# A cast of weights, a low part and a pair of transposes put earlier or later at the entry to the up-projection of block two

## The chip, the cores and the metric

The kernel runs on one core of a Trainium2 chip. The metric is the device time in microseconds (us), the median of three runs. All rows come from one profiled execution. TensorE is called PE here, its weight loads PEld, VectorE DVE, ScalarE ACT, GpSimd POOL and SyncE SP, as in the rows.

## The reference, cut to what matters

The program is a two-block transformer on 256 tokens of width 1024 in float32. Block two has two layers, and each of them ends with a cross-attention to a memory and an MLP:

```
h = rms_norm_2(x, g[2])
y = memory_cross_attention(h, mem, xa_wq[l], xa_wkv[l], xa_wo[l], xa_mem_norm[l])
x = x + rms_norm_2(y, g[3])
h = rms_norm_2(x, g[4])
y = sq_relu_mlp(h, mlp_w1[l], mlp_w2[l])     # square(relu(h @ w1)) @ w2, 1024 -> 4096 -> 1024
```

The entry is the stretch from the cross-attention's last product, with `w_o` (256 x 1024), to the first products with `mlp_w1`. It runs twice, once for each layer. Between the two products lie a norm of `y`, an addition to `x`, and a turning (transposition) of `x`, since PE needs the features on the partitions.

## The kernel before

**Numbers and weights.** A float32 product is computed as three products of reduced float32 (fp32r): high by high, high by low, low by high. So each weight and each activation is split: ACT casts the high part, and DVE (for some halves POOL) subtracts it to get the low part. Weights stream from HBM through three raw buffers in chunks of 128 x 2048, each handled as two halves of 128 x 1024. Half `m` gets its high part in slot `m % 4` of `whi` (`HL` is 4), its low part in the same slot of `wlo`. ACT does the casts of the halves strictly in order: `split_half(k)` casts all halves up to number k that aren't cast yet. A cast into a slot must wait until PE has used up the half that was there before:

```
if m >= HL:
    act.wait_ge(pe_out, 2 * (m - HL + 1))
nc.scalar.copy(whi[:, m % HL, 0:w], raw[...]).then_inc(hi_done, 1)
```

PE adds two to `pe_out` for each half of weights that it has used up. With `n0` the first half of the job `out2`, the halves are: `n0 + 10, 11` for `w_q`; `n0 + 12, 13` for `w_o`; `n0 + 14, 15` for the first 256 columns of `mlp_w1` (step 0); `n0 + 16, 17` for the next 256 (step 1). Half `n0 + 16` takes the slot of half `n0 + 12`.

**Tokens.** The 256 tokens are two tiles (`tt` 0 and 1) of 128, and the 1024 features are eight blocks of 128, taken as four groups (`g` 0 to 3) of two.

**PE.** `cross_out(tt, c)` computes tile tt, columns 512c to 512c+511 of `y`, with six products: for each half `h` of `w_o` the lines L1997, L1998 and L1999. `w_o` is needed for all four of (0,0), (0,1), (1,0), (1,1), so only the last of them gives its halves back. In (1,1) the products L1998 and L1999 with half h add one each to `pe_out`, so half `n0 + 12` is given back by the third of the six products, and `n0 + 13` by the sixth:

```
if tt == c == 1:
    m0.then_inc(pe_out, 1)
    m1.then_inc(pe_out, 1)
```

Then comes `first_up()`. In it `turn_to(tt, g)` transposes two blocks of `x` (L1323, two instructions) once DVE has added that half of the tile's row to `x`; `spare` issues fillers (L1329); `high(step, tt, g, fs)` issues the products of high weights with both parts of the activations (L2034; two blocks of features for each block of 128 columns in `fs`); `low_weights(step, g)` those of the low weights (L2044). `high` of step 0 waits for `grp_dve`, which tells that DVE has made group g's low part, and `high` also for the cast of its half. `turn_to(1, 0)` and `turn_to(1, 1)` use the PSUM banks of groups 2 and 3 of tile 0, so they come behind those groups' low parts.

**ACT.** `cross_square(tt, c)` (L2645) sums squares of `y` for the norm; it waits for PE's product of that piece. `up_hi(tt, g)` (L2653, two instructions) makes the high part of a turned group.

**DVE.** `gain(tt, c)` (L3651) multiplies `y` by its gain and waits for the square of the same piece; `mean(tt)` (L3656) joins both sums of squares of a tile, for which POOL then takes the root (L939); `add(tt, c)` (L3662) adds the normed piece to `x`; `up_lo(tt, g)` (L3670, two instructions) makes the low part of a turned group out of `up_hi`'s result.

**POOL** behind the two roots: it waits for the last addition to `x`, loads a row of gains, and makes the low parts of halves `n0 + 16, 17` (L949). **SP** issues a chunk's load when both parts of the chunk three before have been made.

Every engine works through its list in the order of the code; nothing is reordered at run time.

Of the kernel before, what the change touches and what calls it, by code (L numbers as in the profile page):

```python
# [204 lines left out]
def build_network(nc, a, out):  # L205
# [66 lines left out]
    with ExitStack() as ctx:  # L272
# [843 lines left out]
        def _(pe):  # L1116
# [607 lines left out]
            for l in range(DEPTH):  # L1724
# [286 lines left out]
                def first_up():  # L2011

                    def turn_to(tt, g):

                        pe.wait_ge(x_ready, x_count("yx", l) - 3 + 2 * tt + g // 2)
                        turn_blocks(("xm", l, tt, g), [x[:, tt, (2 * g + b) * P:(2 * g + b + 1) * P] for b in range(2)])

                    def weights(step, g):

                        m = 2 * plan.jobs["w1", l, step][0] + g // 2  # L2020
                        return m, [w[:, m % HL, :].rearrange("p (k n) -> p k n", k=KD // 2) for w in (whi, wlo)]

                    def high(step, tt, g, fs=(0, 1)):

                        m, (wh, _) = weights(step, g)
                        if tt == 0 and g % 2 == 0:
                            pe.wait_ge(hi_done, m + 1)
                        if step == 0:
                            pe.wait_ge(grp_dve, plan.by_number[plan.groups["xm", l, tt, g]][2])
                        rows_ = slice(tt * P, tt * P + P)  # L2030
                        for f in fs:
                            both = ps[:, step_bank(step) + f, :].rearrange("p (i n) -> p i n", i=2)[:, :, rows_]
                            for k in (2 * g, 2 * g + 1):
                                nc.tensor.matmul(both, wh[:, k % 4, f * P:f * P + P], act2[:, k, :, rows_], start=k == 0 and tt == 0, stop=False)  # L2034

                    def low_weights(step, g):

                        m, (_, wl) = weights(step, g)
                        if g % 2 == 0:
                            wait_lo(pe, m)  # L2040
                        for f in range(2):
                            top = ps[:, step_bank(step) + f, 0:SEQ]
                            for k in (2 * g, 2 * g + 1):
                                mm = nc.tensor.matmul(top, wl[:, k % 4, f * P:f * P + P], act2[:, k, 0], start=False, stop=k == KD - 1)  # L2044
                            if g % 2:
                                mm.then_inc(pe_out, 1)

                    for g in range(3):
                        turn_to(0, g)
                    spare(2, 7)  # L2050
                    high(0, 0, 0)
                    high(1, 0, 0, (0,))
                    turn_to(0, 3)
                    high(0, 0, 1)
                    high(1, 0, 0, (1,))
                    high(1, 0, 1)
                    high(0, 0, 2)
                    turn_to(1, 0)
                    high(1, 0, 2)
                    high(0, 0, 3)  # L2060
                    turn_to(1, 1)
                    high(1, 0, 3)
                    for g in range(4):
                        high(0, 1, g)
                        if g < 2:
                            turn_to(1, g + 2)
                        low_weights(0, g)
                        high(1, 1, g)
                    for g in range(4):
                        low_weights(1, g)  # L2070
# [52 lines left out]
        def _(act):  # L2123
# [8 lines left out]
            def split_half(m_last):  # L2132

                while n_split[0] <= min(m_last, 2 * NCH - 1):
                    m = n_split[0]
                    n, h = divmod(m, 2)
                    kc, cols, _ = plan.chunks[n]
                    w = kc // 2 * cols
                    if m == 0:
                        act.wait_ge(first_half_in, 16)  # L2140
                        nc.scalar.copy(whi[:, 0, 512:w], raw[:, 0, 512:w]).then_inc(hi_done, 1)
                        n_split[0] += 1
                        continue
                    elif m == 2:
                        act.wait_ge(second_half_in, 16)
                    elif h == 0 or m in (1, 3):
                        act.wait_ge(landed[n % RAW], plan.landed[n])
                    if m >= HL:

                        act.wait_ge(pe_out, 2 * (m - HL + 1))  # L2150
                    nc.scalar.copy(whi[:, m % HL, 0:w], raw[:, n % RAW, h * w:h * w + w]).then_inc(hi_done, 1)  # L2151
                    n_split[0] += 1
# [153 lines left out]
            for l in range(DEPTH):  # L2306
# [59 lines left out]
                n0 = 2 * plan.jobs["out1", l, 1][0]  # L2366
# [22 lines left out]
                for b in range(NFB):  # L2389
                    g, m = NFB * l + b, 2 * plan.jobs["up", l, b][1]  # L2390
# [17 lines left out]
                n0 = 2 * plan.jobs["down", l, NFB - 1][-1]  # L2408
# [19 lines left out]
            for l in range(DEPTH):  # L2428
# [52 lines left out]
                n0 = 2 * plan.jobs["in2", l, order[0]][0]  # L2481
# [19 lines left out]
                if even:  # L2501
                    n0 = 2 * plan.jobs["out2", l, 0][0]
# [138 lines left out]
                def cross_square(tt, c):  # L2641

                    wait_cross_out(act, l, tt, c)
                    at = 2 * c + tt
                    nc.scalar.activation(junk_act[:, at, :], ps[:, yxb(tt, c), :], ACT.Square, scale=D ** -0.5,  # L2645
                                         accum_out=ss[:, NORM["yx", l], at:at + 1]).then_inc(ss_ready, 1)

                def up_hi(tt, g):

                    key, row = ("xm", l, tt, g), gain_row["xm", l]  # L2650
                    group_ready(act, key)
                    for b in range(2):
                        ins = nc.scalar.activation(ahi[:, 2 * g + b, tt * P:tt * P + P], ps[:, bank_of(key), b * P:b * P + P], ACT.Copy,  # L2653
                                                   scale=gains[:, 2 * g + b, row:row + 1])
                    ins.then_inc(grp_act, 1)
# [4 lines left out]
                cross_hi(1)  # L2660
                cross_square(0, 0)
                cross_square(0, 1)
                cross_square(1, 0)
                split_half(n0 + 16)
                up_hi(0, 0)
                cross_square(1, 1)
                for g in (1, 2, 3):
                    up_hi(0, g)
                split_half(n0 + 17)
                for g in range(4):  # L2670
# [33 lines left out]
        def _(dve):  # L2704
# [605 lines left out]
            for l in range(DEPTH):  # L3310
# [385 lines left out]
                after(n)  # L3696
                add(0, 0)
                add(0, 1)
                gain(1, 0)
                up_lo(0, 0)  # L3700
                mean(1)
                n = gain(1, 1)
                for g in (1, 2, 3):
                    up_lo(0, g)
                    if g > 1:
                        if g == 2:
                            dve.wait_ge(rstd_ready, rs_count["yx second", l])
                            after(n)
                        add(1, g - 2)
# [75 lines left out]
```

## Time and profile before

| | us |
|---|---|
| median of 3 runs | 1346.4 (1346.31 to 1346.7) |
| the profiled execution's own time | 1346.09 |
| its span, first to last instruction | 1344.2 |
| PE busy in the span | 1334.3 (99%) |
| DVE busy | 974.3 (72%) |
| ACT busy | 740.2 (55%) |
| entry of layer 0, first products of the up-projection | 869.27 |
| entry of layer 1, the same | 1160.25 |

A row of the timeline gives start, duration, engine, line, operation, output and inputs, and how many instructions are merged in it; a bracket at its end says how long the engine had been idle and whose work ended the idle time. Durations of instructions that follow each other on one engine overlap somewhat, so the distance from one start to the next is what one costs in a queue. The ends of matmuls are modelled.

### The profile page before, as it was taken

The page shows a single profiled execution, that of the slowest core. Times are in us where ns is not written, and L with a number is a line of the kernel's source. Part 1 is how long each engine was busy: PE and PEld are TensorE (multiplying, and loading weights), DVE is VectorE, ACT ScalarE, POOL GpSimd, SP SyncE. Part 2 cuts the span into 40 slices and gives each one's busy share as a digit, 9 for nine tenths or more (in the row PEclk, how much of TensorE's full clock was granted, in tenths as well). Part 3 has the DMA queues.
Part 4 walks back from the last instruction along what each step waited for, and adds up shares of the span by engine and source line. Part 5 has one row for each costly group of instructions (what it writes and reads, how often), then busy time and mean ns, then how long its engine had stood idle before and what let it go on. Part 6 is the DMA issues. An engine that isn't in the chain of part 4 may idle for free.

```text
span 1344.2 us, 19217 instructions
## 1 busy us (share of the span) xinstructions
PE 1334.3 (99%) x7365; PEld 1121.7 (83%) x7365; DVE 974.3 (72%) x1502; ACT 740.2 (55%) x1155; POOL 125.3 (9%) x114
## 2 busy tenths in 40 slices
PE   9999999999999999999999999999999999999998
PEld 6888888888888888888888777888888878888886
DVE  7566878777664767877778687886667887786665
ACT  6564555554545754555445676754445675654443
POOL 1000011111000000311111002220000010400000
PEclk9999999999999999999999999999999999999999
DMA  9743545555455334656655524357765524355552
GB/s 375 246 153 129 187 158 193 187 195 192 173 219 186 127 126 160 228 200 231 202 189 201 170 95 151 117 216 227 216 204 193 182 79 173 119 206 193 191 191 88
DMA packets 37673, 244.32 MB, mean 182 GB/s; under 512 B 4656, under 2 KB 5312, under 8 KB 10192
## 3 DMA queue, kind: packets, MB, share of 16 engines
q1 hardware_dynamic: 33568, 228.08, 47.9%
q0 software_dynamic: 3728, 14.82, 3.9%
q8 instruction: 59, 0.97, 0.3%
q14 instruction: 30, 0.25, 0.1%
q10 hardware_dynamic: 288, 0.21, 0.1%
HBM read 241.13 MB, written 1.97 MB: 181 GB/s over the span
## 4 chain that ended last, share of the span: by engine, by line
PE 97%; DVE 1%; ACT 1%; DMA 0%; issue 0%; POOL 0%; ACTq 0%; DVEq 0%
PE ps L1217 19%; PE ps L1155 17%; PE ps L1161 16%; PE ps L1164 16%; PE ps L1224 10%; PE ps L1323 3%; PE ps L1418 2%; PE ps L1449 2%; PE ps L1400 1%; PE ps L2034 1%; PE ps L1265 1%; PE ps L1259 1%; PE ps L1262 1%; PE ps L1577 1%; PE ps L2044 1%; PE ps L1578 1%
## 5 line engine op out<-in xcount | busy, mean ns | idle before, releaser
L2736 DVE TENSOR_TENSOR wlo<-raw,whi 128x1024 fp32r<-128x1024 f32 (+2 forms) x423 | 510.4, 1217 | 264.2 <-ACT whi L2151 263.1
L2151 ACT CAST whi<-raw 128x1024 fp32r<-128x1024 f32 (+1 forms) x431 | 444.6, 1041 | 332.9 <-PE ps L1224 188.5
L1217 PE MATMUL ps<-act,whi 128*128 128x512 f32 x1120 | 266.4, 390 | 0.0
L1217 PEld LDWEIGHTS ps<-act,whi 128*128 128x128 f32 x1120 | 208.4, 188 | 42.2
L1155 PE MATMUL ps<-whi,mhi 128*128 128x512 f32 (+2 forms) x688 | 235.7, 392 | 0.3 <-DVE mlo L2760 0.3
L1161 PE MATMUL ps<-wlo,mhi 128*128 128x512 f32 (+2 forms) x688 | 231.1, 385 | 0.0
L1164 PE MATMUL ps<-whi,mlo 128*128 128x512 f32 (+2 forms) x688 | 231.0, 385 | 0.0
L1164 PEld LDWEIGHTS ps<-whi,mlo 128*128 128x128 f32 x688 | 129.2, 188 | 26.4
L1161 PEld LDWEIGHTS ps<-wlo,mhi 128*128 128x128 f32 x688 | 129.2, 188 | 26.1 <-DVE wlo L2736 0.5
L1224 PEld LDWEIGHTS ps<-act,wlo 128*128 128x128 f32 x1120 | 143.6, 191 | 5.5
L1155 PEld LDWEIGHTS ps<-whi,mhi 128*128 128x128 f32 x688 | 125.9, 188 | 24.1 <-issue 2.4
L1224 PE MATMUL ps<-act,wlo 128*128 128x256 f32 x1120 | 145.3, 283 | 0.0
L1155 PE MATMUL ps<-whi,act 128*128 128x512 f32 (+1 forms) x336 | 126.3, 376 | 0.0
L1164 PE MATMUL ps<-whi,act 128*128 128x512 f32 (+1 forms) x336 | 124.1, 369 | 0.0
L1161 PE MATMUL ps<-wlo,act 128*128 128x512 f32 (+1 forms) x336 | 124.0, 369 | 0.0
L1155 PEld LDWEIGHTS ps<-whi,act 128*128 128x128 f32 x336 | 63.3, 188 | 11.7 <-ACT whi L2151 0.8
L1005 POOL TENSOR_TENSOR work<-work 128x512 f32<-128x512 f32 x22 | 48.4, 2200 | 257.8 <-DVE work L3138 250.0
L1164 PEld LDWEIGHTS ps<-whi,act 128*128 128x128 f32 x336 | 63.3, 188 | 10.9
L1161 PEld LDWEIGHTS ps<-wlo,act 128*128 128x128 f32 x336 | 63.4, 189 | 10.1
L939 POOL TENSOR_TENSOR rstd<-ss,small 128x2 f32<-128x2 f32 (+1 forms) x22 | 19.4, 880 | 490.8 <-DVE ss L3288 166.8
L2214 ACT ACTIVATE work<-work,low 128x128 f32<-128x128 f32 (+3 forms) x80 | 40.8, 512 | 28.3 <-DVE low L2830 24.1
L2691 ACT CAST mhi<-work 128x512 fp32r<-128x512 f32 x32 | 19.9, 621 | 66.0 <-DVE work L3737 66.0
(334 smaller groups left out, 1516.3 us busy)
## 6 DMA issues: line engine op xcount, KB each, us to landing
raw<-in_weights SPq DMA_DIRECT2D x210, 1024.0 KB, 4.8
gain_b<-in_norm_g POOLq DMA_DIRECT2D x6, 512.0 KB, 4.0
raw<-in_weights SPq DMA_DIRECT2D x5, 512.0 KB, 5.8
region<-in_b_gate POOLq DMA_DIRECT2D x2, 1024.0 KB, 8.6
o_nat<-in_mem_turned POOLq DMA_DIRECT2D x2, 1024.0 KB, 7.2
region<-band POOLq DMA_DIRECT2D x8, 256.0 KB, 5.0
region<-band POOLq DMA_DIRECT2D x8, 192.0 KB, 5.9
x<-in_x SPq DMA_DIRECT2D x1, 1024.0 KB, 11.6
```

The lines of the kernel that those rows point to most:

```text
L1005: nc.gpsimd.tensor_tensor(two(up_as), two(up_a), row, ALU.mult).then_inc(a_scaled, 1)
L1155: nc.tensor.matmul(o, hi[:, kx, rows_], wh[:, k, c0:c0 + w], start=first and h == 0 and k == 0 and (tt == 0 or at[1] == 0), stop=False)
L1161: nc.tensor.matmul(o, hi[:, kx, rows_], wl[:, k, c0:c0 + w], start=False, stop=False)
L1164: mm = nc.tensor.matmul(o, lo[:, kx, rows_], wh[:, k, c0:c0 + w], start=False, stop=final and h == 1 and k == kh - 1 and (tt == 1 or at[1] ...
L1217: nc.tensor.matmul(ps[:, bank0 + f, :], of(whi, h)[:, k, f * P:f * P + P], act2[:, kx].rearrange("p i n -> p (i n)"), start=kx == 0, stop= ...
L1224: mm = nc.tensor.matmul(ps[:, bank0 + f, 0:SEQ], of(wlo, h)[:, k, f * P:f * P + P], act2[:, kx, 0], start=False, stop=kx == KD - 1)
L1323: mm = nc.tensor.transpose(bank[:, j * P:j * P + P], src, ident)
L1418: mm = nc.tensor.transpose(turned(u, d)[:, at:at + P], step_of(1536, u, d)[:, at:at + P], ident)
L1449: mm = nc.tensor.matmul(ps[row:row + HD, d["o_bank"], d["o_col"]:d["o_col"] + P], d["pv"][b], values_of(u, d)[:, b * P:(b + 1) * P], start ...
L2151: nc.scalar.copy(whi[:, m % HL, 0:w], raw[:, n % RAW, h * w:h * w + w]).then_inc(hi_done, 1)
L2214: nc.scalar.activation(step_of(1536, u, d), step_of(0, u, d), ACT.Exp, scale=-1.0, bias=low[:, d["qt"], s:s + 1], accum_out=den[:, d["qt"] ...
L2736: nc.vector.tensor_tensor(wlo[:, m % HL, 0:w], raw[:, n % RAW, h * w:h * w + w], whi[:, m % HL, 0:w].bitcast(F32), ALU.subtract).then_inc( ...
```

## The change

It is made in three lists of instructions, for both layers alike; no instruction is added or removed.

- ACT: the cast of half `n0 + 16` stands ahead of `cross_square(1, 0)` instead of behind it, and `up_hi(0, 1)` ahead of `cross_square(1, 1)`.
- DVE: `up_lo(0, 0)` stands ahead of `gain(1, 0)`, and `up_lo(0, 1)` ahead of `mean(1)` and `gain(1, 1)`.
- PE: `turn_to(0, 2)` stands behind the first six products instead of ahead of the fillers.

```
@@ PE
-                    for g in range(3):
+                    for g in range(2):
                         turn_to(0, g)
                     spare(2, 7)
                     high(0, 0, 0)
                     high(1, 0, 0, (0,))
+                    turn_to(0, 2)
                     turn_to(0, 3)
                     high(0, 0, 1)
@@ ACT
                 cross_square(0, 0)
                 cross_square(0, 1)
+                split_half(n0 + 16)
                 cross_square(1, 0)
-                split_half(n0 + 16)
                 up_hi(0, 0)
+                up_hi(0, 1)
                 cross_square(1, 1)
-                for g in (1, 2, 3):
+                for g in (2, 3):
                     up_hi(0, g)
                 split_half(n0 + 17)
@@ DVE
                 add(0, 0)
                 add(0, 1)
+                up_lo(0, 0)
                 gain(1, 0)
-                up_lo(0, 0)
+                up_lo(0, 1)
                 mean(1)
                 n = gain(1, 1)
-                for g in (1, 2, 3):
+                for g in (2, 3):
                     up_lo(0, g)
```

ACT at the entry of layer 0, before, from the squares of pieces (0,0), (0,1) and (1,0) on (L2151 is the cast, L2653 the high parts):

```order
L2645 ACTIVATE work,ss<-ps 128x512 [waits wo_out] x3
L2151 CAST whi<-raw 128x1024 [waits pe_out,landed1]
L2653 ACTIVATE act<-ps,gains 128x128 [waits pe_grp]
L2653 ACTIVATE act<-ps,gains 128x128
L2645 ACTIVATE work,ss<-ps 128x512 [waits pe_out]
L2653 ACTIVATE act<-ps,gains 128x128 [waits pe_grp]
```

The same place of the changed kernel (its lines are numbered one higher here):

```order
L2646 ACTIVATE work,ss<-ps 128x512 [waits wo_out] x2
L2152 CAST whi<-raw 128x1024 [waits pe_out,landed1]
L2646 ACTIVATE work,ss<-ps 128x512 [waits wo_out]
L2654 ACTIVATE act<-ps,gains 128x128 [waits pe_grp]
L2654 ACTIVATE act<-ps,gains 128x128
L2654 ACTIVATE act<-ps,gains 128x128 [waits pe_grp]
L2654 ACTIVATE act<-ps,gains 128x128
L2646 ACTIVATE work,ss<-ps 128x512 [waits pe_out]
```

The cast, which waits for `pe_out`, now stands between the second and the third square, and two groups of high parts stand together ahead of the fourth.

DVE at the same entry, before, from the two additions of tile 0 on:

```order
L3662 SCALAR_TENSOR_TENSOR x<-work,rstd,x 128x512 [waits chain,rstd_ready]
L3662 SCALAR_TENSOR_TENSOR x<-work,rstd,x 128x512
L3651 TENSOR_TENSOR work<-ps,gain_b 128x512 [waits ss_ready,wo_out]
L3670 SCALAR_TENSOR_TENSOR act<-ps,gains,act 128x128 [waits grp_act]
L3670 SCALAR_TENSOR_TENSOR act<-ps,gains,act 128x128
L3656 SCALAR_TENSOR_TENSOR ss<-ss 128x1 [waits ss_ready]
L3651 TENSOR_TENSOR work<-ps,gain_b 128x512 [waits ss_ready,pe_out]
```

And in the changed kernel (lines two higher):

```order
L3664 SCALAR_TENSOR_TENSOR x<-work,rstd,x 128x512 [waits chain,rstd_ready]
L3664 SCALAR_TENSOR_TENSOR x<-work,rstd,x 128x512
L3672 SCALAR_TENSOR_TENSOR act<-ps,gains,act 128x128 [waits grp_act]
L3672 SCALAR_TENSOR_TENSOR act<-ps,gains,act 128x128
L3653 TENSOR_TENSOR work<-ps,gain_b 128x512 [waits ss_ready,wo_out]
L3672 SCALAR_TENSOR_TENSOR act<-ps,gains,act 128x128 [waits grp_act]
L3672 SCALAR_TENSOR_TENSOR act<-ps,gains,act 128x128
L3658 SCALAR_TENSOR_TENSOR ss<-ss 128x1 [waits ss_ready]
```

The low part of group 0 has moved ahead of the product of tile 1's first piece with its gain, and that of group 1 ahead of the mean.

PE at the same entry, before, from the first pair of transposes on:

```order
L1323 MATMUL ps<-cst,x 128x128 [waits grp_act,x_ready]
L1323 MATMUL ps<-cst,x 128x128
L1323 MATMUL ps<-cst,x 128x128 [waits grp_act,x_ready]
L1323 MATMUL ps<-cst,x 128x128
L1323 MATMUL ps<-cst,x 128x128 [waits grp_dve,x_ready]
L1323 MATMUL ps<-cst,x 128x128
L1329 MATMUL ps<-ident_b 128x512 x2
L2034 MATMUL ps<-act,whi 128x2x128 [waits grp_dve,hi_done]
L2034 MATMUL ps<-act,whi 128x2x128 x3
L2034 MATMUL ps<-act,whi 128x2x128 [waits hi_done]
L2034 MATMUL ps<-act,whi 128x2x128
L1323 MATMUL ps<-cst,x 128x128 [waits grp_dve,x_ready]
```

And in the changed kernel, from the second pair on:

```order
L1323 MATMUL ps<-cst,x 128x128 [waits grp_act,x_ready]
L1323 MATMUL ps<-cst,x 128x128
L1329 MATMUL ps<-ident_b 128x512 x2
L2034 MATMUL ps<-act,whi 128x2x128 [waits grp_dve,hi_done]
L2034 MATMUL ps<-act,whi 128x2x128 x3
L2034 MATMUL ps<-act,whi 128x2x128 [waits hi_done]
L2034 MATMUL ps<-act,whi 128x2x128
L1323 MATMUL ps<-cst,x 128x128 [waits grp_dve,x_ready]
L1323 MATMUL ps<-cst,x 128x128
L1323 MATMUL ps<-cst,x 128x128 [waits grp_dve,x_ready]
L1323 MATMUL ps<-cst,x 128x128
L2034 MATMUL ps<-act,whi 128x2x128 [waits grp_dve]
```

Two pairs of transposes instead of three stand ahead of the fillers, and two instead of one between the first six products and the next.

## Rows read from the trace of the kernel before

**Rows 1.** The page: the span and its instructions, and PE's busy time.
```profile
span 1344.2 us, 19217 instructions
...
PE 1334.3 (99%) x7365; PEld 1121.7 (83%) x7365; DVE 974.3 (72%) x1502; ACT 740.2 (55%) x1155; POOL 125.3 (9%) x114
```

**Rows 2.** All waits of PE: who waited for whom, total, times, longest.
```profile
PE ps L2034 <- DVE act L3670: 1.0, 2, 0.5
```

**Rows 3.** Timeline, layer 0's entry, PE: start, us, instructions, idle time before.
```profile
865.74 0.39 PE L1999 MATMUL ps<-whi,mlo 128*128 128x512 f32 x1
...
866.42 0.39 PE L1999 MATMUL ps<-whi,mlo 128*128 128x512 f32 x1
...
867.34 0.98 PE L1323 MATMUL ps<-cst,x 128*128 128x128 f32 x6
...
867.87 0.20 PEld L1323 LDWEIGHTS ps<-cst,x 128*128 128x128 f32 x2 [0.18 <-DVE x L3662]
...
869.27 0.95 PE L2034 MATMUL ps<-act,whi 128*128 128x256 f32 x6 [0.52 <-DVE act L3670]
...
870.06 0.38 PE L1323 MATMUL ps<-cst,x 128*128 128x128 f32 x2
...
870.44 1.95 PE L2034 MATMUL ps<-act,whi 128*128 128x256 f32 x14
...
872.22 0.38 PE L1323 MATMUL ps<-cst,x 128*128 128x128 f32 x2
...
872.36 1.20 PE L2034 MATMUL ps<-act,whi 128*128 128x256 f32 x8
```

**Rows 4.** Timeline of the same stretch, ACT.
```profile
866.17 0.60 ACT L2645 ACTIVATE work<-ps 128x512 f32<-128x512 f32 x1 [0.67 <-PE ps L1999]
...
866.90 1.05 ACT L2151 CAST whi<-raw 128x1024 fp32r<-128x1024 f32 x1
867.86 0.62 ACT L2653 ACTIVATE act<-ps,gains 128x128 fp32r<-128x128 f32 x2
868.37 0.60 ACT L2645 ACTIVATE work<-ps 128x512 f32<-128x512 f32 x1
...
868.94 1.16 ACT L2653 ACTIVATE act<-ps,gains 128x128 fp32r<-128x128 f32 x4
870.48 0.63 ACT L2653 ACTIVATE act<-ps,gains 128x128 fp32r<-128x128 f32 x2 [0.38 <-PE ps L1323]
```

**Rows 5.** Timeline of the same stretch, DVE.
```profile
866.41 1.42 DVE L3662 SCALAR_TENSOR_TENSOR x<-work,rstd,x 128x512 f32<-128x512 f32 x2
...
868.51 0.61 DVE L3670 SCALAR_TENSOR_TENSOR act<-ps,gains,act 128x128 fp32r<-128x128 f32 x2
...
869.17 0.69 DVE L3651 TENSOR_TENSOR work<-ps,gain_b 128x512 f32<-128x512 f32 x1
869.78 1.12 DVE L3670 SCALAR_TENSOR_TENSOR act<-ps,gains,act 128x128 fp32r<-128x128 f32 x4
870.82 0.74 DVE L3662 SCALAR_TENSOR_TENSOR x<-work,rstd,x 128x512 f32<-128x512 f32 x1
871.48 0.60 DVE L3670 SCALAR_TENSOR_TENSOR act<-ps,gains,act 128x128 fp32r<-128x128 f32 x2
872.00 0.74 DVE L3662 SCALAR_TENSOR_TENSOR x<-work,rstd,x 128x512 f32<-128x512 f32 x1
```

**Rows 6.** POOL's two low parts of step 1's weights, in the timeline; ACT's later cast.
```profile
873.66 4.75 POOL L949 TENSOR_TENSOR wlo<-raw,whi 128x1024 fp32r<-128x1024 f32 x2
...
890.58 1.05 ACT L2151 CAST whi<-raw 128x1024 fp32r<-128x1024 f32 x1
```

**Rows 7.** The page's DMA issues: size, and us from issue to landing.
```profile
raw<-in_weights SPq DMA_DIRECT2D x210, 1024.0 KB, 4.8
```

**Rows 8.** Stretches: busy time (instructions) of each engine, PE's granted clock, DMA share, GB/s.
```profile
868.00:870.00 2.00, 1.48 (x10) 1.00 (x11) 1.91 (x6) 2.00 (x8) 0.56 (x1) 1.00 0.31 131
...
1340.00:1344.20 4.20, 0.00 (x0) 0.00 (x0) 1.65 (x3) 0.00 (x0) 0.24 (x1) 0.63 0.59 227
```

More of the change, by code:

```diff
@@ L2046, in low_weights @@
                                 mm.then_inc(pe_out, 1)
-                    for g in range(3):
+                    for g in range(2):
                         turn_to(0, g)
@@ L2052, in first_up @@
                     high(1, 0, 0, (0,))
+                    turn_to(0, 2)
                     turn_to(0, 3)
@@ L2662, in _ @@
                 cross_square(0, 1)
+                split_half(n0 + 16)
                 cross_square(1, 0)
-                split_half(n0 + 16)
                 up_hi(0, 0)
+                up_hi(0, 1)
                 cross_square(1, 1)
-                for g in (1, 2, 3):
+                for g in (2, 3):
                     up_hi(0, g)
@@ L3698, in _ @@
                 add(0, 1)
+                up_lo(0, 0)
                 gain(1, 0)
-                up_lo(0, 0)
+                up_lo(0, 1)
                 mean(1)
                 n = gain(1, 1)
-                for g in (1, 2, 3):
+                for g in (2, 3):
                     up_lo(0, g)
```

## The prediction

> **What bounds the kernel now.** First the page: PE is busy 1334.3 us of a span of 1344.2 [rows 1], so only what makes PE wait or work longer changes the time, and all its idle time together is 10 us. Then the list of PE's waits: the entry is in it, twice, with 1.0 us in total, and it is DVE's low part (L3670) that ends the wait [rows 2]. Two equal entries mean that I can work one out and double it. Then the timeline of the entry of layer 0, engine by engine. On PE six transposes start at 867.34, the last pair of them held 0.18 us by an addition to x; the fillers follow; then PE stands still for 0.52 us until 869.27, when the first products may start [rows 3]. What ends this hole is a chain, to be read backwards through the engines: the low part of group 0 starts on DVE at 868.51 [rows 5], the high part of it on ACT at 867.86, and ahead of that on ACT stands the cast, from 866.90, though the transposes of group 0 began at 867.34 and could have been taken earlier [rows 3, 4]. So the cast is what the first products wait for. From 870.44 on PE is fed: 14 products take 870.44 to 872.22, 0.127 us each [rows 3].
>
> **When the cast may start.** The change wants the cast in ACT's idle time of 0.67 us ahead of the third square [rows 4], from 865.50 on. But its half (n0 + 16) goes into the slot of half n0 + 12, the first half of w_o, and PE gives that back only with the third of the six products of the last piece (1,1). That product starts at 866.42 [rows 3]. How long after a product's start ACT moves, the third square shows: the last product of its piece starts at 865.74 [rows 3] and the square at 866.17 [rows 4], 0.43 us later. So the cast is released at 866.85, and before it ran from 866.90: at its old place it had just nothing to wait for. Moved ahead, it starts at 866.85 all the same, ACT idles with it at the head of its list, and the third square, ready at 866.17, is queued behind it.
>
> **Part by part, layer 0's entry.** Prices in a queue are distances of starts.
>
> ACT. Cast 866.85; a cast costs 0.96 (866.90 to 867.86), so the third square starts at 867.81; a square costs 0.57 (868.37 to 868.94), so the high part of group 0 starts at 868.38 instead of 867.86; the two groups cost 0.51 each (867.86 to 868.37), so group 1's starts at 868.89 and the fourth square at 869.40 [rows 4].
>
> DVE. The low part follows the high part by 0.65 (867.86 to 868.51) [rows 4, 5]: 869.03. The gain of piece (1,0), now behind it, also waits for the late third square, but that costs nothing, since DVE is busy with the low part until 869.55 (0.52 a group, 871.48 to 872.00); the gain costs 0.61 (869.17 to 869.78), so group 1's low part starts at 870.16 [rows 5].
>
> PE. Products follow a low part's start by 0.76 (868.51 to 869.27), or by 0.66 where it was the first of two (869.78 to 870.44) [rows 3, 5]. First products: 869.79, **0.52 later** than before. Six of them take 0.79 (869.27 to 870.06) [rows 3]. Then stand two pairs of transposes instead of one. A pair's price is read from the three pairs before: the third pair's load stands at 867.87, held 0.18, its transposes some 0.1 behind it, the first pair's at 867.34, so two pairs take 867.87 + 0.1 - 0.18 - 867.34 = 0.45, 0.22 each; products follow the last pair by 0.14 (872.22 to 872.36) [rows 3]. Transposes of group 2 at 870.58, of group 3 at 870.80, the next products at 870.94; group 1's low part would have let them go at 870.82 and is not what they wait for. Before they began at 870.44: **0.50 later**. The pair taken out of the hidden stretch is thus paid in full, but before these products also waited for DVE some 0.2 (pair to product 0.38 instead of 0.14 [rows 3]), which is saved, and the two cancel.
>
> Group 2. Before, its low part was ready long ahead. Now its transposes start at 870.58; ACT follows transposes by 0.42 (870.06 to 870.48) [rows 3, 4]: 871.00; DVE by 0.65: 871.65; PE by 0.76: 872.41. PE would come to these products ten products behind 870.94, at 872.21, against 871.71 before. So PE waits again, and is **0.70 later**.
>
> Tile 1. The addition (1,0) stands behind group 2's low part on DVE: 871.65 + 0.52 = 872.17, and ends 0.74 later, at 872.91; before it started at 870.82 and was done long before PE came [rows 5]. Its release reaches PE within about 0.1: the two additions of tile 0 end at 867.83 [rows 5], and PE's load of the waiting pair starts at 867.87 [rows 3], the transposes a tenth behind their load. So the transposes of (1,0) start at 873.05 instead of 872.22, **0.83 later**. The mean and the gain of (1,1) (fourth square done at about 870.1, mean at 870.7, gain to 871.4) are in time for it, and so is POOL's root. Behind this, the chain transposes, high part, low part, products is 0.42 + 0.65 + 0.76 = 1.83 with nothing in its way (the addition (1,1) leaves DVE at 874.1, just when the low part of (1,0) wants it), and the products in between are the same as before, so the lateness stays 0.83.
>
> POOL and SP. The last addition ends at about 874.1 instead of 872.74 (872.00 + 0.74) [rows 5], so POOL's two low parts, 873.66 to 878.41 [rows 6], come 1.4 later, and with them SP's load of the chunk three on, at 879.8; 4.8 us to landing [rows 7] makes 884.6, and the cast that needs it ran at 890.58 [rows 6]. Nothing; were that cover gone, every 1 us would cost 1.
>
> Sum: 0.83 x 2 = 1.7 us. Nothing behind the entry absorbs it, since PE has no other wait there. Against the profiled execution, 1346.09, that is 1347.8; the median of the runs is 0.3 above it: **1348.1**.
>
> Bounds. Below: the terms of group 2 and of tile 1 are small differences of long sums; without them 0.50 an entry, 1.0 in all. Above: cast at 866.90 (0.05), the square in front of the high part at its full busy time with its reading, 0.69 instead of 0.57 (0.12), another 0.1 where queues meet: 1.1 an entry, 2.2 in all. So 1347.4 to 1348.6, and 0.3 for the spread of runs.
>
> The hole on PE grows from 0.52 to 1.4 us, since the fillers run 0.4 earlier (a pair's 0.22 and the 0.18 of its hold). The rows show a granted clock of 1.00 (2.4 GHz) over the present hole; it falls only behind the last product, to a mean of 0.63 over 1340 to 1344.2, in which PE has no instruction at all [rows 8]. I take it to stay. The Trainium skill (TensorE: Matmul & The Clock Gate, Part 1: The HAM clock gate) says that the throttled state is the default one and that activity lifts it, so a longer hole could bring it back; by that the sum would grow as in the third rival, and no run here shows yet whether a hole of 1.4 us does it.
>
> **Rivals.**
> 1. The cast is not held (the slot is free earlier than I read it). Then cast 865.50, third square 866.46; the high part of group 0 waits only for its transposes, 867.34 + 0.42 = 867.76; low part 868.41; first products 869.17, 0.1 earlier. Next ones 870.31, 0.13 earlier. But group 2, turned at 869.96, is ready for PE at 871.79 against 871.71, and the addition (1,0) then ends at 872.29, the transposes come at 872.43: 0.2 later. In all +0.4, 1346.8. For it speaks that ACT shows no wait at the cast; against it the 0.43, which fits to 0.05.
> 2. A gain: the saved waits on PE outweigh all else. Even if both waits at both entries were gone (0.52 + 0.24, twice) it would be 1.5 us: 1344.9. Against it: the chain above has no shorter path.
> 3. Slower by over 2.7 us: the hole lowers the clock. 1.35 an entry is needed, 0.5 more than my sum, which is 0.5 us of products at 1.2 GHz. If the products from 869.8 up to the transposes of (1,2), some 4 us, ran at half rate, it would be 4 us an entry, 1356. For it the longer hole, against it clocks of 1.00 over the present hole [rows 8].
>
> **Chances.** A measurement of this kernel tells some 0.2%, 2.7 us, from no change. My forecast 0.76 (1347.1 to 1348.9); rival 1 0.14 (1346.3 to 1347.1); rival 2 0.04; rival 3 0.04; a longer chain than summed 0.02, half of it beyond 2.7. Only rival 3 and that half are slower by over 0.2%; 0.01 stays for faster by as much, which rival 2's bound of 1.5 us all but excludes. The range leaves out rivals 2 and 3 and the lower edge of rival 1: 1346.6 to 1349.0.
>
> **What would show it.** Right: ACT's cast starts at about 866.85 with idle time of about 1.3 before it, released by PE's L1999; the third square at 867.8; the hole on PE before its first products about 1.4 and these at 869.8; a second small wait of PE for L3670 ahead of group 2's products, and the transposes of tile 1 at 873.0. Wrong: a cast at 865.5 (rival 1), a granted clock under 1.00 at 869 to 875 (rival 3), or first products before 869.27.

## The result and the profile after

| | us |
|---|---|
| before, median | 1346.39 (1346.01 to 1347.53, 21 runs) |
| changed, median | 1348.16 (1347.88 to 1349.23, 21 runs) |
| ratio | 1.0014, 95% interval 1.0008 to 1.0020 |
| forecast | 1348.1, range 1346.6 to 1349.0 |

The changed kernel is 1.8 us slower. That is less than the 0.2% named ahead as what counts as a change, but the interval leaves out 1.

The page of the changed kernel has the same instructions and the same busy PE as [rows 1], in a span 2.0 us longer, so nearly all that was added is waiting:

```profile
span 1346.2 us, 19217 instructions
...
PE 1334.2 (99%) x7365; PEld 1121.9 (83%) x7365; DVE 975.0 (72%) x1502; ACT 740.0 (55%) x1155; POOL 125.3 (9%) x114
```

PE's waits, the row that answers to [rows 2] (lines of the changed kernel stand two higher on DVE): 3.0 us instead of 1.0, 1.5 for each entry.

```profile
PE ps L2034 <- DVE act L3672: 3.0, 2, 1.5
```

PE's timeline at layer 0's entry, to be laid beside [rows 3]. The whole stretch stands 0.11 us later than there, and so do w_o's products ahead of it (866.53 against 866.42), so this shift comes from earlier in the program:

```profile
866.53 0.39 PE L1999 MATMUL ps<-whi,mlo 128*128 128x512 f32 x1
...
867.44 0.60 PE L1323 MATMUL ps<-cst,x 128*128 128x128 f32 x4
867.88 0.59 PE L1329 MATMUL ps<-ident_b 128*128 128x512 bf16 x2
869.95 0.94 PE L2034 MATMUL ps<-act,whi 128*128 128x256 f32 x6 [1.48 <-DVE act L3672]
870.74 0.60 PE L1323 MATMUL ps<-cst,x 128*128 128x128 f32 x4
871.09 2.19 PE L2034 MATMUL ps<-act,whi 128*128 128x256 f32 x14
873.14 0.44 PE L1323 MATMUL ps<-cst,x 128*128 128x128 f32 x2
```

The hole of 0.52 has become 1.48. The first products start 0.57 later (869.95 less 869.27 less 0.11), those behind the transposes 0.54 later, the transposes of tile 1 0.81 later. PE's second small wait, ahead of group 2's products, isn't in the list of waits and lies hidden among the 14 products from 871.09 on, which take 2.05 instead of 1.78 us up to the next transposes. The weight loads of the same products show it as a gap of 0.23, behind ten loads and ahead of the last four, which are group 2's. The row names no releaser, but the time fits the low part of group 2 (871.81 below, and 0.76 from a low part to its products):

```profile
872.54 0.53 PEld L2034 LDWEIGHTS ps<-act,whi 128*128 128x128 f32 x4 [0.23 <-issue]
```

ACT at the same place, beside [rows 4]:

```profile
864.92 0.60 ACT L2646 ACTIVATE work<-ps 128x512 f32<-128x512 f32 x1 [0.69 <-PE ps L1999]
...
867.01 1.05 ACT L2152 CAST whi<-raw 128x1024 fp32r<-128x1024 f32 x1 [1.41 <-PE ps L1999]
867.97 0.59 ACT L2646 ACTIVATE work<-ps 128x512 f32<-128x512 f32 x1
...
868.55 1.13 ACT L2654 ACTIVATE act<-ps,gains 128x128 fp32r<-128x128 f32 x4
869.55 0.62 ACT L2646 ACTIVATE work<-ps 128x512 f32<-128x512 f32 x1
...
871.15 1.14 ACT L2654 ACTIVATE act<-ps,gains 128x128 fp32r<-128x128 f32 x4 [0.89 <-PE ps L1323]
```

The cast is first in ACT's list from 865.6 on and doesn't start until 867.01: idle 1.41 us, ended by PE's product with the first half of w_o. The third square, whose data were there at about 866.3, runs behind it.

DVE, beside [rows 5]: the low part of group 2 (871.81) now waits for its high part, and the addition (1,0) follows it at 872.34.

```profile
869.20 0.61 DVE L3672 SCALAR_TENSOR_TENSOR act<-ps,gains,act 128x128 fp32r<-128x128 f32 x2 [1.27 <-ACT act L2654]
869.72 0.68 DVE L3653 TENSOR_TENSOR work<-ps,gain_b 128x512 f32<-128x512 f32 x1
870.32 0.60 DVE L3672 SCALAR_TENSOR_TENSOR act<-ps,gains,act 128x128 fp32r<-128x128 f32 x2
...
871.81 0.61 DVE L3672 SCALAR_TENSOR_TENSOR act<-ps,gains,act 128x128 fp32r<-128x128 f32 x2 [0.23 <-ACT act L2654]
872.34 0.74 DVE L3664 SCALAR_TENSOR_TENSOR x<-work,rstd,x 128x512 f32<-128x512 f32 x1
```

**A stage's length.** The entry is short, and its length repeats to 0.02 us between the two layers and between two executions of one kernel (all but those with the cast held longer), so I compare one length in all kernels: on PE, from the start of the first transposes (L1323, 867.34 before) to the start of the pair that spreads the next norm's row behind the last product of step 1 (L1233, 882.18 before). It leaves out whatever moved earlier in the program.

| kernel | layer 0 | layer 1 | both, against before | median of runs, against before |
|---|---|---|---|---|
| before | 14.84 | 14.82 | | |
| changed | 15.71 | 15.72 | +1.77 | +1.77 |
| cast alone | 15.50 | 15.51 | +1.35 | +1.26 |
| pair alone | 15.14 | 15.14 | +0.62 | +0.53 |
| reordered parts alone | 14.82 | 14.82 | -0.02 | -0.11 |
| all but the cast | 15.13 | 15.14 | +0.61 | +0.56 |
| changed, slot sooner | 15.05 | 15.04 | +0.43 | +0.45 |
| group 1 only | 14.60 | 14.61 | -0.45 | -0.41 and -0.48 |
| group 1 and slot sooner | 14.65 | 14.65 | -0.36 | -0.37 |
| changed, held longer | 16.33 | 17.57 | +4.24 | +5.35 |
| the same again | 16.34 | 17.50 | +4.18 | +4.17 |
| held longer, hole filled | 16.34 | 16.33 | +3.01 | +3.07 |

What the two entries lengthen by is what the whole program lengthens by, to 0.1 us, in all but one row; nothing behind the entry absorbs it. The intervals of the single medians below are some 0.1% wide each way, so the verdicts on the parts, of 0.4 to 1.3 us, rest on this stage and on the rows; no single median proves one. The exception is the first profile of the kernel with the cast held longer, and is explained there.

### The profile page after: what moved, and what is told of

Read it like the earlier page. It is cut to its first block, busy times and chain, and to the rows that moved or that the text cites. A ratio compares the mean times of both kernels' runs of the same rounds, so it can differ in the third digit from the quotient of the medians.

```text
span 1346.2 us, 19217 instructions
## 1 busy us (share of the span) xinstructions
PE 1334.2 (99%) x7365; PEld 1121.9 (83%) x7365; DVE 975.0 (72%) x1502; ACT 740.0 (55%) x1155; POOL 125.3 (9%) x114
## 3 DMA queue, kind: packets, MB, share of 16 engines
q0 software_dynamic: 3728, 14.82, 4.0%
HBM read 241.13 MB, written 1.97 MB: 181 GB/s over the span
## 4 chain that ended last, share of the span: by engine, by line
PE 97%; DVE 1%; ACT 1%; DMA 0%; issue 0%; POOL 0%; ACTq 0%; DVEq 0%
PE ps L1217 19%; PE ps L1155 17%; PE ps L1161 16%; PE ps L1164 16%; PE ps L1224 10%; PE ps L1323 3%; PE ps L1418 2%; PE ps L1449 2%; PE ps L1400 1%; PE ps L2034 1%; PE ps L1265 1%; PE ps L1262 1%; PE ps L1259 1%; PE ps L1577 1%; PE ps L2044 1%; PE ps L1579 1%
```

## The experiments

**The cast alone.** The kernel before with

```
                 cross_square(0, 1)
+                split_half(n0 + 16)
                 cross_square(1, 0)
-                split_half(n0 + 16)
```

> The kernel before, with the cast alone moved ahead of the third square on ACT; PE and DVE keep their order. Theory (the cast is held by the slot of w_o's first half, and the third square and the high part queue behind it): the cast starts where it started before, about 0.43 us behind the third product of piece (1,1); the high part of group 0 is 0.52 us later; the gain of piece (1,0), which still stands ahead of group 0's low part on DVE, waits for the late square, so the first products come 0.60 later and the transposes of tile 1 0.58 later: +1.2 us in all. Rival A (the pair of transposes behind the first products costs all of it): 0. Rival B (DVE's new order costs it): 0.

Measured: 1347.66 us, +1.26, ratio 1.0009 (0.9999 to 1.0019). PE's third product of piece (1,1), then ACT's cast, then the first products, each from its engine's timeline:

```profile
866.99 0.39 PE L1999 MATMUL ps<-whi,mlo 128*128 128x512 f32 x1
...
870.56 0.95 PE L2034 MATMUL ps<-act,whi 128*128 128x256 f32 x6 [1.25 <-DVE act L3670]
```

```profile
867.47 1.05 ACT L2151 CAST whi<-raw 128x1024 fp32r<-128x1024 f32 x1 [1.41 <-PE ps L1999]
```

And on DVE the gain of (1,0), which in the kernel before had run in idle time, waits for the late square with group 0's low part behind it:

```profile
869.20 0.69 DVE L3651 TENSOR_TENSOR work<-ps,gain_b 128x512 f32<-128x512 f32 x1 [0.82 <-ACT work L2645]
869.81 0.60 DVE L3670 SCALAR_TENSOR_TENSOR act<-ps,gains,act 128x128 fp32r<-128x128 f32 x2
```

The cast's move costs this by itself; rivals A and B both gave 0. From the first transposes to the first products it is 2.66 us (867.90 to 870.56) instead of 1.93, so 0.73 more where 0.60 was expected.

**The pair of transposes alone.** The kernel before with

```
-                    for g in range(3):
+                    for g in range(2):
                         turn_to(0, g)
                     spare(2, 7)
                     high(0, 0, 0)
                     high(1, 0, 0, (0,))
+                    turn_to(0, 2)
                     turn_to(0, 3)
```

> The kernel before, with the transposes of group 2 alone moved behind the first products on PE. Theory: first products at 869.27 as before, the next at 870.42 (before 870.44), but group 2's parts come 0.42 + 0.65 + 0.76 behind its transposes, 0.18 late, and the addition (1,0) behind them 0.31 late: +0.6 us in all. Rival A (this pair is the whole cost): +1.7. Rival B (DVE's order): 0.

Measured: 1346.93 us, +0.53, ratio 1.0005 (0.9996 to 1.0015). On DVE the low part of group 2 waits, and the addition (1,0) follows it; here the stretch stands 0.39 later than in the kernel before, so the addition is 0.85 late (872.06 less 870.82 [rows 5] less 0.39).

```profile
871.53 0.61 DVE L3671 SCALAR_TENSOR_TENSOR act<-ps,gains,act 128x128 fp32r<-128x128 f32 x2 [0.76 <-ACT act L2654]
872.06 0.74 DVE L3663 SCALAR_TENSOR_TENSOR x<-work,rstd,x 128x512 f32<-128x512 f32 x1
```

PE absorbs most of that and passes on 0.3 an entry. The pair itself, 0.22 us of PE's time, is not what costs: the products behind it stood just where they had, at 870.83 less 0.39. That the rest is group 2's late parts and the addition behind them is read from these rows; no run moved that addition alone.

**The reordered parts alone.** The kernel before with the move of `up_hi(0, 1)` on ACT and both moves of `up_lo` on DVE, cast and transposes as they were:

```
                 up_hi(0, 0)
+                up_hi(0, 1)
                 cross_square(1, 1)
-                for g in (1, 2, 3):
+                for g in (2, 3):
                     up_hi(0, g)
@@ DVE
+                up_lo(0, 0)
                 gain(1, 0)
-                up_lo(0, 0)
+                up_lo(0, 1)
                 mean(1)
                 n = gain(1, 1)
-                for g in (1, 2, 3):
+                for g in (2, 3):
                     up_lo(0, g)
```

> The kernel before, with only the reorderings of parts: the high part of group 1 ahead of the fourth square on ACT, the low part of group 0 ahead of the gain of (1,0) and that of group 1 ahead of the mean on DVE. Cast and transposes stay. Theory: the first products stay at 869.27, the next come 0.14 earlier, the addition (1,0) is later and just in time: 0.0 in all, -0.1 to +0.1. Rival A: 0. Rival B: +1.7.

Measured: 1346.29 us, -0.11, ratio 0.9998 (0.9989 to 1.0007). Rival B falls. PE's timeline shows the products behind the transposes 0.23 behind these (870.20 to 870.43) instead of 0.38 [rows 3], and the time is lost again at the transposes of tile 1, which are held: the products behind them start 0.20 after them (872.27 to 872.47) instead of 0.14.

**All but the cast.** The changed kernel with the cast put back behind `cross_square(1, 0)`.

> The changed kernel with the cast alone put back behind the third square. Theory: first products at 869.27, the next at 870.42, group 2's 0.18 late, the transposes of tile 1 0.31 late: +0.6 us against the kernel before, 1.1 less than the changed kernel. Rival A: +1.7. Rival B: +1.7.

Measured: 1346.96 us, +0.56, ratio 1.0006 (0.9997 to 1.0016). It is the pair alone over again; the reordered parts neither help nor harm it. So of the 1.8 us the cast is 1.2 and the pair 0.6. In the stage, cast alone and pair alone sum to 1.35 + 0.62 = 1.97, the changed kernel to 1.77: with the cast alone the gain of (1,0) stood between the late square and the low part (the 0.82 above), and the first products came 2.66 us behind the first transposes; in the changed kernel the low part goes first, and it is 2.51 (867.44 to 869.95).

**The slot given back sooner.** The changed kernel with tile 1 of the product with w_o half by half:

```
-                def cross_out(tt, c):
+                def cross_out(tt, c, hs=(0, 1)):
...
-                    for h in range(2):
+                    for h in hs:
...
-                cross_out(1, 0)
-                cross_out(1, 1)
+                cross_out(1, 0, (0,))
+                cross_out(1, 1, (0,))
+                cross_out(1, 0, (1,))
+                cross_out(1, 1, (1,))
```

> The changed kernel, but PE computes tile 1 of the product with w_o half by half: the first half for (1,0) and (1,1), then the second half for both. So the first half's slot is given back by the sixth of these twelve products instead of the ninth, 0.68 us sooner, and the piece (1,0) is done 0.68 later. Theory: the cast starts 0.68 sooner, 0.43 behind that sixth product, the third square behind it has its data by then, the high part of group 0 waits for its transposes alone, and the first products come 0.6 us sooner than in the changed kernel: 1.3 us under the changed kernel, +0.4 against the kernel before (the pair's price, as in the run of the pair alone). Rival (the cast moved ahead is late for a reason of its own, its DMA or the low parts, and not for the slot): it starts as late as in the changed kernel, and the third square too: +1.7 or more.

Measured: 1346.85 us, +0.45, ratio 1.0004 (0.9995 to 1.0013). The sixth of the twelve products on PE, with the first products behind, and the cast on ACT:

```profile
865.98 0.39 PE L1999 MATMUL ps<-whi,mlo 128*128 128x512 f32 x1
...
869.41 0.95 PE L2034 MATMUL ps<-act,whi 128*128 128x256 f32 x6 [0.80 <-DVE act L3674]
```

```profile
866.46 1.05 ACT L2154 CAST whi<-raw 128x1024 fp32r<-128x1024 f32 x1 [0.73 <-PE ps L1999]
```

The cast followed the product that frees its slot, 0.48 behind it as in the changed kernel, and the 1.3 us came back. This is the direct proof of the hold: nothing on ACT or DVE was touched, nor the load of the raw weights, and the only other effect of the edit, a later piece (1,0), could not have made anything sooner.

**Group 1 only.** The kernel before with

```
                 up_hi(0, 0)
+                up_hi(0, 1)
                 cross_square(1, 1)
-                for g in (1, 2, 3):
+                for g in (2, 3):
                     up_hi(0, g)
@@ DVE
                 gain(1, 0)
                 up_lo(0, 0)
+                up_lo(0, 1)
                 mean(1)
                 n = gain(1, 1)
-                for g in (1, 2, 3):
+                for g in (2, 3):
                     up_lo(0, g)
```

> The kernel before, with the high part of group 1 ahead of the fourth square on ACT and the low part of group 1 ahead of the mean and the gain of (1,1) on DVE, and nothing else. The gain of (1,0) keeps its free place in DVE's idle time, so the addition (1,0) isn't late. Theory: first products as before, the products behind the transposes of group 3 no longer wait 0.24 us for group 1's low part, and nothing takes it back: -0.5 us in all, 1345.9. Rival (whatever DVE saves there, the additions of tile 1 lose): 0.0, as with the reorderings that also moved the gain.

Measured: 1345.99 us, -0.41, ratio 0.9996 (0.9987 to 1.0005). The products behind the transposes of group 3 start 0.13 behind them, without the wait of [rows 3]:

```profile
869.72 0.94 PE L2034 MATMUL ps<-act,whi 128*128 128x256 f32 x6 [0.52 <-DVE act L3671]
870.50 0.38 PE L1323 MATMUL ps<-cst,x 128*128 128x128 f32 x2
870.63 1.91 PE L2034 MATMUL ps<-act,whi 128*128 128x256 f32 x14
```

The same kernel once more:

> The kernel with the two moves of group 1 alone, once more, to narrow its interval: 0.4 us under the kernel before, as it was the first time, if the gain is real; 0 if it was the chance of one batch.

Measured: 1345.88 us, -0.48, ratio 0.9994 (0.9985 to 1.0003). Both intervals include 1, so the medians alone don't prove the gain. But both sets of runs gave it, and the stage is shorter by 0.21 to 0.24 in each of the four entries profiled. By the medians it is 0.03% faster than the kernel before, and so the fastest of these kernels.

**Group 1, and the slot sooner.** The kernel before with the two moves of group 1, `cross_out` half by half and the cast ahead of the third square.

> The kernel before with the two moves of group 1, and also tile 1 of the product with w_o computed half by half and the cast ahead of the third square. Theory: the cast then costs nothing there, the high part of group 0 comes 0.1 sooner, but its low part stands behind the gain of (1,0), which waits for the third square: 0.05 sooner an entry than without it, -0.6 us against the kernel before. Rival (slot not the cause): the cast is still late, +0.5 or more.

Measured: 1346.03 us, -0.37, ratio 0.9997 (0.9988 to 1.0006). The cast costs nothing now, but the further gain expected, 0.1 in all, isn't there; in the stage it is 0.09 worse than group 1 only. The high part of group 0 did come 0.10 sooner (0.42 behind the first transposes instead of 0.52). But the gain of (1,0) had to wait for the later square, and group 0's low part, which stands behind it on DVE, started 1.23 us behind the first transposes instead of 1.17.

**The cast held longer.** The changed kernel with

```
                 cross_square(0, 1)
+                act.wait_ge(pe_out, 2 * (n0 + 14))
                 split_half(n0 + 16)
```

> The changed kernel with one wait more on ACT: the cast ahead of the third square also waits until PE has given back w_o's second half, which its sixth product of piece (1,1) does, 0.68 us behind the third. Theory (the hold is the cost and PE pays all of it): the cast, the third square, the high part of group 0 and PE's first products all come 0.68 later than in the changed kernel, so does tile 1: +1.4 us against it, +3.1 against the kernel before. Rival (the cast isn't on the path, something else in the new order is): no more than the changed kernel, +1.7.

Measured: 1351.71 us, +5.35, ratio 1.0033 (1.0021 to 1.0045). The hold did what was expected of it: layer 0's entry is 0.62 longer than the changed kernel's, where 0.68 was expected. But 5.35 isn't 3.1, and layer 1's entry is 1.85 longer. So there is a second cost, and the list of stretches shows it in PE's clock. Hence two kernels more: this one again, and one with

```
-                    spare(2, 7)
+                    spare(9, 7)
```

> The kernel with the cast held 0.68 us longer, once more, beside the one with the fillers. If the surplus is the clock, each of the two entries either loses 1.3 us or doesn't, and the runs stand near 1349.5, 1350.8 and 1352.0; if not, they stand together.

> The kernel with the cast held 0.68 us longer, and nine fillers on PE ahead of the first products instead of two. Seven more at 0.21 us each (512 columns, two of them took 0.44 from start to start of what followed) take 1.5 us of the hole of 2.1 us that this kernel had, and end before the first products can start. Theory that the surplus over 3.1 us was PE's clock, which fell to a mean of 0.57 to 0.58 over 1164 to 1168 behind the hole in layer 1's entry: with the hole filled the clock stays at 1.00 and the time is the +3.1 us of the hold alone, 1349.5. Rival (the surplus belongs to the hold, in a queue, or to the start of the program): 1351.5, as without the fillers.

Measured, without added fillers: 1350.42 us, ratio 1.0030 (1.0018 to 1.0041); its runs stand at 1349.21, 1349.34, 1350.41, 1350.44, 1351.61 and 1351.75. With fillers: 1349.32 us, ratio 1.0021 (1.0012 to 1.0031), all eleven runs from 1349.14 to 1349.38. PE at layer 1's entry without added fillers, then stretches of 2 us (busy time and instructions of PE, PEld, DVE, ACT, POOL, then PE's granted clock):

```profile
1163.13 1.62 PE L2034 MATMUL ps<-act,whi 128*128 128x256 f32 x6 [2.10 <-DVE act L3673]
1164.55 1.05 PE L1323 MATMUL ps<-cst,x 128*128 128x128 f32 x4
1165.26 2.45 PE L2034 MATMUL ps<-act,whi 128*128 128x256 f32 x14
```

```profile
870.00:872.00 2.00, 1.39 (x12) 1.42 (x13) 2.00 (x7) 1.10 (x5) 0.27 (x1) 1.00 0.03 8
...
1162.00:1164.00 2.00, 0.87 (x4) 0.90 (x5) 1.62 (x5) 1.44 (x6) 0.00 (x0) 0.76 0.00 0
1164.00:1166.00 2.00, 2.00 (x11) 2.00 (x11) 0.89 (x4) 0.79 (x4) 0.56 (x1) 0.50 0.03 8
1166.00:1168.00 2.00, 2.00 (x17) 2.00 (x16) 2.00 (x6) 1.33 (x4) 0.00 (x0) 0.89 0.00 0
```

And with fillers, the same place:

```profile
1160.51 2.11 PE L1329 MATMUL ps<-ident_b 128*128 128x512 bf16 x9
1163.21 0.94 PE L2034 MATMUL ps<-act,whi 128*128 128x256 f32 x6 [0.60 <-DVE act L3673]
1164.00 0.60 PE L1323 MATMUL ps<-cst,x 128*128 128x128 f32 x4
1164.35 2.19 PE L2034 MATMUL ps<-act,whi 128*128 128x256 f32 x14
```

```profile
1162.00:1164.00 2.00, 1.40 (x10) 0.91 (x8) 1.54 (x5) 1.52 (x6) 0.00 (x0) 1.00 0.00 0
1164.00:1166.00 2.00, 1.95 (x17) 1.77 (x16) 1.77 (x6) 1.58 (x5) 0.56 (x1) 1.00 0.04 8
```

Behind a hole of 2.10 us six products took 1.42 us from their start to that of the transposes (1163.13 to 1164.55), behind one filled down to 0.60 they took 0.79: the clock had gone to 0.50, 1.2 GHz, and came back within the stretch to 1168. It cost layer 1's entry 1.2 us (17.50 against 16.34 at layer 0's entry, where a hole as long, 2.11, left the clock at 1.00). Both entries' holes are equally long, and no run here tells why the one is hit and not the other. The three levels of the runs, 1.2 apart, fit none, one or two such falls in an execution, and the mean granted clock recorded for each run agrees: 1.000 and 1.000 at 1349.2 to 1349.3, 0.998 and 0.998 at 1350.4, 0.997 and 0.997 at 1351.6 to 1351.8. With the fillers it was 0.999 or 1.000 in all eleven.

In the first set of runs of this kernel they stood at the two upper levels (1350.41, 1350.57, and three from 1351.71 to 1351.94). Its profiled run, 1351.71, has one slowed entry and a second fall at the start of the program, behind a wait of PE of 1.85 us for its first activations:

```profile
6.79 0.90 PE L1528 MATMUL ps<-whi,act 128*128 128x512 f32 x2 [1.85 <-ACT act L2185]
7.49 1.05 PE L1528 MATMUL ps<-wlo,act 128*128 128x512 f32 x2
...
8.00:10.00 2.00, 2.00 (x6) 1.55 (x5) 2.00 (x5) 2.00 (x5) 0.00 (x0) 0.50 1.04 417
```

In the kernel before, the first of these rows starts at 6.46 and the two products of the second row take 0.63. So a stretch at half the clock need not lie at the entries, and this one explains why 5.35 is 1.1 more than the two entries' 4.24: the first transposes of layer 0 already start 1.36 later than in the kernel before (868.70 against 867.34). For the runs without a profile the place of the falls isn't shown (and one of that set, 1350.57, has a mean clock of 1.000, so the match of levels and clocks isn't strict). Why every run of that set had at least one stays open.

## Why the prediction was right

The forecast was 1348.1 and the median is 1348.16. By its steps, for layer 0 with the shift of 0.11 taken off:

| step | forecast | measured |
|---|---|---|
| cast starts | 866.85 | 866.90 |
| third square | 867.81 | 867.86 |
| high part of group 0 | 868.38 | 868.44 |
| first products | 869.79 | 869.84 |
| next products | 870.94 | 870.98 |
| high part of group 2 | 871.00 | 871.04 |
| transposes of tile 1 | 873.05 | 873.03 |
| lateness passed on, an entry | 0.83 | 0.87 and 0.90 |
| POOL's low parts | 1.4 later | 1.42 later (875.19 less 873.66 less 0.11) |

- **The hold** was the step on which the rest stood. It is shown in three ways: the cast moved ahead alone doesn't start sooner, it starts sooner when its slot is given back sooner, and later when it is made to wait for the next half.
- **One term was mis-sized.** The release was put at 0.43 us behind the third product, from a square's start. The cast follows its product by 0.48 or 0.49 in every kernel but the longer hold (0.42 to 0.44 there), the kernel before included (866.42 to 866.90). So the cast hadn't "just nothing to wait for" at its old place: it was held there too. [rows 4] shows this in the distances of starts, 0.73 from the square to the cast (866.17 to 866.90) against 0.57 from a square to what follows it (868.37 to 868.94). The timeline puts no idle time in front of the cast, because the square is followed by the reading of its sum, which ends at 866.85:

```profile
866.66 0.19 ACT L2645 ACTIVATION_READ_ACCUMULATOR work<-ps 128x1 f32 x1
866.90 1.05 ACT L2151 CAST whi<-raw 128x1024 fp32r<-128x1024 f32 x1
```

  The error of about 0.05 goes through all steps from the cast to group 2's high part; the bounds had a term of this size for it. That it is down to -0.02 at tile 1, and that the median lies within 0.06 us of the forecast, is luck beyond what the sum could promise.
- **The transposes.** The pair behind the first products was priced as cancelling against the saved wait, with group 2's late parts as the true cost. The pair alone bears that out: next products unmoved, 0.3 an entry passed on. The second small wait ahead of group 2's products was there, too (the load's 0.23).
- **Tile 1.** The addition behind group 2's low part came as forecast. But the lateness did not stay at 0.83: the products behind the transposes of tile 1 started 0.19 behind them instead of 0.14 (873.14 to 873.33), so 0.87 and 0.90 an entry went on.
- **Rival 1**, cast not held, would have been 1346.8; with the slot given back sooner the kernel is at 1346.85, so its sum was right and only its condition wasn't met. Its steps fit too: counted from the first transposes, first products 0.09 earlier than in the kernel before (forecast 0.1), transposes of tile 1 0.15 later (forecast 0.2).
- **Rival 2** bounded any gain at this place by 1.5 us; the part of it that could be had, group 1's wait, is 0.4.
- **Rival 3**, the clock, was right as a mechanism and wrong for this hole. In the changed kernel the holes of 1.48 us leave it at 1.00 at both entries, and the six products behind them take 0.79 us as before (869.95 to 870.74):

```profile
868.00:870.00 2.00, 0.52 (x4) 0.08 (x1) 0.80 (x3) 2.00 (x8) 0.00 (x0) 1.00 0.35 147
...
1160.00:1162.00 2.00, 0.52 (x3) 0.16 (x2) 0.88 (x3) 2.00 (x8) 0.00 (x0) 1.00 0.33 139
```

  Its price was put at 4 us an entry; measured it is 1.2, since the clock stood at 0.50 behind the hole only until about 1166.4 (an estimate from the mean of 0.89 over 1166 to 1168), some 3.3 us, where a loss of 4 us would have needed 8. The Trainium skill (TensorE: Matmul & The Clock Gate, Part 1: The HAM clock gate) has the throttled state as the default that activity lifts; the runs with the longer hold agree, with clocks of 0.50 behind an idle PE and of 1.00 where fillers kept it busy, though layer 0's hole of 2.11 us left it at 1.00 as well.

## What to carry to other kernels

Before an instruction is moved into an engine's idle time, ask for each of its waits when it is met, and not only whether its data are there: a wait that is met by chance at the old place holds the whole queue at the new one. A short wait can be missing from the profile's idle time (here some 0.16 us by the starts), so compare the distance of starts with that of the same instruction and its follower elsewhere, and the start with the release. And where a hole on PE grows, read the granted clock behind it and not only its length.

## What the runs showed that was not expected

- A hole of 2.1 us on PE took the clock to 0.50 at one entry and not at the other of the same execution, in both profiles of this kernel, at a price of 1.2 us beyond the hole. Seven more fillers took the price away and made the runs stand within 0.24 us of each other instead of 2.5.
- The distance from the product that frees a slot to the cast that waits for it was the same 0.48 or 0.49 us in the kernel before, the changed one and the seven other kernels in which the third product of a piece frees it, while a square follows the last product of its piece by 0.43. It isn't a matter of cast or square: where the cast was made to wait for the last product of piece (1,1), it followed by 0.42 to 0.44, too. What makes the 0.05 between a piece's third product and its last, no run tells.
- PE's wait for its first activations at the program's start ranged from 0.5 to 1.9 us among the profiled runs of kernels that are alike there, but the products behind it started within 0.65 us of each other (6.46 to 7.11). What cost more was a slow stretch behind it. In the second profile of the kernel with group 1's moves alone two products that take 0.63 us in the kernel before took 1.05:

```profile
7.62 1.05 PE L1528 MATMUL ps<-wlo,act 128*128 128x512 f32 x2
```

  The granted clock reads 1.00 there, and that run is 1.1 us above its kernel's median, at 1347.01. The kernel before, too, has three runs of 16 in one set at 1347.6 to 1348.0, 1.3 to 1.7 above the median; whether they are of this kind isn't shown. So a clock of 1.00 in the rows isn't enough, the distances of the products have to be compared as well, and a single profiled time can be off by nearly the whole effect studied; the length of the stage was not, but for the clock.
